# Last FFN of a decoder trunk: gate and value tile as seven products of quarters, and one projection moved

## The chip, the cores and the metric

The kernel runs on one NeuronCore of a Trainium2 chip. The metric is the device time of one launch in microseconds. Engines: PE (TensorE), DVE (VectorE), ACT (ScalarE), POOL (GpSimd), SP (SyncE, which issues the DMAs).

## The reference

One inference step of a two-layer recurrent decoder trunk in float32: model width 1024, 1024 prompt tokens and 8 sample tokens, all with the same weights.

```
for layer in (0, 1):
    x += mixer(rmsnorm(x, norm_mix[layer]))      # layer 0: gated linear attention + retention
                                                 # layer 1: mLSTM + RG-LRU; each ends in ... @ w_out
    g, u = split(rmsnorm(x, norm_ffn[layer]) @ w_up)   # 1024 -> 2 x 2816
    x += (silu(g) * u) @ w_down                        # 2816 -> 1024
y = rmsnorm(x, norm_final)
```

The mixer states of the prompt and of the samples are outputs too.

## The kernel before, in words

Everything is transposed: features on partitions, tokens on the free axis. The tokens are two sets, A (512 prompt tokens) and B (512 prompt tokens and the 8 samples, 520, worked as two pieces of 260 columns, each in a PSUM bank of its own). A tensor of width 1024 is eight tiles of 128 rows.

Every product is split: a float32 operand is a high part (an fp32r copy, by ACT) and a low part (the operand less its high part, by POOL for weights and by DVE for activations), and a product is high x high + high x low + low x high, three matmuls. Weights come in blocks of 128 x 1024 (512 KB) through a ring of four slots: SP fills `wr` (line 594) once the block four before is used, ACT makes `wh` (L1114), POOL `wl` (L1380).

An FFN has 22 hidden tiles, worked as 11 groups of two. A group has four `up` units (gate, value, gate, value; `dense`, L761), each eight k-steps x 3 matmuls, for B x 2 pieces, and then eight `down` units of the group before it (L816), each two k-steps x 3, for B x 2 pieces. A `down` unit is added to `x` by DVE (`accumulate`, L1774). The gate's way: DVE multiplies the PSUM result by the norm's factor `rs` into `sq` (L1550), ACT applies Silu (L1239), POOL multiplies by `rs` once more (L1486), DVE multiplies with the value's PSUM result into `hf` (L1787), ACT makes `hidh` (L1244), DVE `hidl` (L1793). So the normalisation by `rs` comes behind the product: the FFN's input is only x times the gain (`x_split`, L1124 and L1563).

`order()` writes one list of steps by hand; every engine walks this list in order and does what the step means for it. `Plan` gives each PE unit one bank of four (B: an aligned pair of banks) in turn, and PE waits, before it writes, until the bank's last user has been read. A step placed between two others on DVE thus also delays what stands behind it.

Layer 1 before: mixer of A, FFN of layer 0 for B, output projection of A, input projections of B, FFN of A (with the mixer's scans of B between its units), output projection `out` of B (8 units of 48 matmuls, with A's final norm and output beside it), FFN of B. The last group of downs of B goes in two halves of the columns, with the final norm between.

## Time and profile before

| | us |
|---|---|
| median of 3 runs | 2498.04 (2495.83 to 2499.22) |
| the profiled execution | 2493.78 |
| its span, first to last instruction | 2492.0 |
| PE busy | 2432.9 (98%) |
| POOL busy | 1252.7 (50%) |
| DVE busy | 1007.6 (40%) |
| ACT busy | 934.2 (37%) |

Busy time of PE is modelled from pipelined matmuls; its weight loads (PEld) lie beside them. A row of a timeline gives start, duration and instruction, and in brackets how long the engine had been idle and who released it; "x2" is two instructions merged. `xB<-ps,xB` means that xB is written from ps and xB. L1774 is a line of the kernel.

### The profile page before, as it was taken

What the parts mean: (1) busy time and instruction counts of PE and PEld (TensorE: products, weight loads), DVE (VectorE), ACT (ScalarE), POOL (GpSimd) and SP (SyncE); (2) the same over time, 40 slices, a digit from 0 to 9 for tenths busy, and PEclk for the clock granted to TensorE, in tenths of its full rate; (3) what the DMA queues carried; (4) which work ended last, traced back from release to release, by engine and by line L of the source; (5) the groups of instructions that cost most, each with busy time, mean ns of one, the idle gap of its engine ahead of it and who ended that gap; (6) DMA issues with size and microseconds to landing.
All of it is one profiled execution on the core that took longest, in us unless ns stands there. A gap on an engine that the chain in (4) does not pass through costs nothing.

```text
span 2492.0 us, 36702 instructions
## 1 busy us (share of the span) xinstructions
PE 2432.9 (98%) x15510; PEld 2193.5 (88%) x15510; DVE 1007.6 (40%) x1712; ACT 934.2 (37%) x1219; POOL 1252.7 (50%) x669
## 2 busy tenths in 40 slices
PE   8999999899999999999999999999999999999998
PEld 6889987688887877999999889988887889999998
DVE  4513245334445434543333443454434454222224
ACT  5342345233223455443333254544432335222223
POOL 3745455555455644544354473344445556544453
PEclk9999999999999999999999999999999999999999
DMA  5322233321323222222222222222233323222222
GB/s 184 102 82 69 71 130 97 115 77 60 123 85 119 92 90 92 88 74 94 85 77 94 77 88 87 85 95 75 86 101 107 126 86 127 92 88 93 94 85 86
DMA packets 74594, 235.18 MB, mean 94 GB/s; under 512 B 9216, under 2 KB 13120, under 8 KB 74432
## 3 DMA queue, kind: packets, MB, share of 16 engines
q1 hardware_dynamic: 74432, 232.84, 27.9%
q8 instruction: 123, 2.02, 0.3%
q14 instruction: 39, 0.32, 0.0%
HBM read 221.64 MB, written 9.05 MB: 93 GB/s over the span
## 4 chain that ended last, share of the span: by engine, by line
PE 86%; DVE 5%; POOL 2%; issue 2%; ACT 2%; POOLq 1%; DVEq 1%; DMA 1%; SPq 0%; ACTq 0%
PE ps L761 62%; PE ps L816 17%; POOL wl L1380 1%; DMA wr<-in_wblk 1%; PE ps L912 1%; PE ps L910 1%; PE ps L856 1%; ACT wh L1114 1%; PE ps L785 0%; DVE sq L1550 0%; DVE mixl L1764 0%; POOL sq L1486 0%; PE ps L973 0%; POOLq L1397 0%; PE ps L970 0%
## 5 line engine op out<-in xcount | busy, mean ns | idle before, releaser
L1380 POOL TENSOR_TENSOR wl<-wr,wh 128x1024 fp32r<-128x1024 f32 x392 | 943.3, 2420 | 592.2 <-ACT wh L1114 591.7
L761 PE MATMUL ps<-xh,wh 128*128 128x260 f32 (+2 forms) x3296 | 882.5, 322 | 8.1 <-DVE qk L1552 4.2
L761 PE MATMUL ps<-xl,wh 128*128 128x260 f32 (+2 forms) x3296 | 869.0, 318 | 0.0
L761 PE MATMUL ps<-xh,wl 128*128 128x260 f32 (+1 forms) x3280 | 867.1, 319 | 0.0
L761 PEld LDWEIGHTS ps<-xh,wh 128*128 128x128 f32 (+1 forms) x3296 | 544.4, 188 | 61.6 <-issue 18.8
L761 PEld LDWEIGHTS ps<-xl,wh 128*128 128x128 f32 (+1 forms) x3296 | 543.7, 188 | 44.9 <-issue 2.4
L761 PEld LDWEIGHTS ps<-xh,wl 128*128 128x128 f32 x3280 | 541.9, 188 | 44.6
L1114 ACT ACTIVATE wh<-wr 128x1024 fp32r<-128x1024 f32 (+2 forms) x396 | 410.0, 1045 | 393.8 <-DMA wr<-in_wblk 389.2
L816 PE MATMUL ps<-hidh,wh 128*128 128x260 f32 (+1 forms) x1024 | 279.9, 327 | 21.8 <-POOL wl L1380 9.5
L1239 ACT ACTIVATE sq<-sq 128x512 f32<-128x512 f32 (+1 forms) x88 | 55.9, 636 | 609.0 <-DVE sq L1550 609.0
L816 PE MATMUL ps<-hidl,wh 128*128 128x260 f32 (+1 forms) x1024 | 276.3, 323 | 0.0
L816 PE MATMUL ps<-hidh,wl 128*128 128x260 f32 (+1 forms) x1024 | 276.0, 323 | 0.0
L816 PEld LDWEIGHTS ps<-hidh,wh 128*128 128x128 f32 x1024 | 171.9, 190 | 44.3 <-issue 13.7
L1486 POOL TENSOR_TENSOR sq<-sq,rsB 128x520 f32<-128x520 f32 x44 | 60.0, 1364 | 296.7 <-ACT sq L1239 296.7
L1486 POOL TENSOR_TENSOR sq<-sq,rsA 128x512 f32<-128x512 f32 x44 | 57.7, 1312 | 273.6 <-ACT sq L1239 273.5
L1774 DVE TENSOR_TENSOR xB<-ps,xB 128x520 f32<-128x520 f32 x184 | 128.5, 699 | 163.3 <-PE ps L816 107.6
L816 PEld LDWEIGHTS ps<-hidh,wl 128*128 128x128 f32 x1024 | 171.4, 190 | 15.6
L816 PEld LDWEIGHTS ps<-hidl,wh 128*128 128x128 f32 x1024 | 171.7, 190 | 14.1
L1774 DVE TENSOR_TENSOR xA<-ps,xA 128x512 f32<-128x512 f32 x192 | 129.1, 687 | 125.2 <-PE ps L816 75.9
L1787 DVE TENSOR_TENSOR hf<-ps,sq 128x512 f32<-128x512 f32 (+1 forms) x88 | 61.0, 693 | 292.3 <-PE ps L761 278.5
L1244 ACT ACTIVATE hidh<-hf 128x512 fp32r<-128x512 f32 (+1 forms) x88 | 55.8, 634 | 214.7 <-DVE hf L1787 214.7
L1550 DVE TENSOR_TENSOR sq<-ps,rsB 128x520 f32<-128x520 f32 x44 | 30.8, 699 | 186.5 <-PE ps L761 180.4
(373 smaller groups left out, 2316.9 us busy)
## 6 DMA issues: line engine op xcount, KB each, us to landing
wr<-in_wblk SPq DMA_DIRECT2D x392, 512.0 KB, 3.4
xr<-in_xT SPq DMA_DIRECT2D x8, 260.0 KB, 5.8
xB<-in_xT SPq DMA_DIRECT2D x8, 260.0 KB, 5.8
out_yT<-xB SPq DMA_DIRECT2D x8, 260.0 KB, 2.2
xr<-in_xT SPq DMA_DIRECT2D x8, 256.0 KB, 6.0
xA<-in_xT SPq DMA_DIRECT2D x8, 256.0 KB, 4.4
Ss<-in_s_even SPq DMA_DIRECT2D x1, 2048.0 KB, 10.1
out_ss_even<-Ss SPq DMA_DIRECT2D x1, 2048.0 KB, 9.2
```

Source lines behind the costliest of these rows:

```text
L761: mm = pe.matmul(ps[0:cols, b + c, 0:n], wt[:, w], xt[:, e:e + n], start=first, stop=end)
L816: mm = pe.matmul(ps[:, b + c, 0:n], wt[:, w], xt[:, t + lo:t + lo + n], start=first, stop=end)
L856: mm = pe.matmul(ps[:, b + c, 0:n], lhsT, src[0:p, lo:lo + n], start=True, stop=True)
L910: pe.matmul(ob, QZ[X][:, h * C:(h + 1) * C], S[:, (h // 2) * P:(h // 2 + 1) * P], start=True, stop=False)
L1114: act.activation(hi, raw, ACT.Copy).then_inc(s_hi, 1)
L1239: act.activation(t, t, ACT.Silu).then_inc(s_si, 1)
L1244: act.activation(hidh[:, t], hf[:, t], ACT.Copy).then_inc(s_hh, 1)
L1380: pool.tensor_tensor(lo, raw, hi.bitcast(F32), ALU.subtract).then_inc(s_lo, 1)
L1486: pool.tensor_tensor(t, t, rs[X][:], ALU.mult).then_inc(s_sr, 1)
L1550: mm = v.tensor_tensor(cut(dst, X), src, cut(rs[X][:], X), ALU.mult)
L1774: v.tensor_tensor(t, bank(pl.bank[u], X), t, ALU.add).then_inc(s_evd, 1)
L1787: v.tensor_tensor(cut(hf[:, t:t + W[X]], X), bank(pl.bank[u], X), cut(sq[q // 2][:, 0:W[X]], X), ALU.mult).then_inc(s_evd, 1)
```

## The change

Only the last FFN of B and its surroundings change.

- A pair (gate tile and value tile of one hidden tile) is a product of 2 x 2 blocks (gate or value; first or second half of the 1024 inputs) with 2 x 2 blocks (halves of the inputs; halves of the columns). It is worked as seven products of quarters (`sp`), each 4 k-steps x 3 matmuls of 260 columns into one bank, in place of eight. The weights of a pair are a set of eight quarters of 512 columns: two blocks by DMA (`wq`, `weight_set`), four quarters from DVE (`wS`, `set_sums`); seven of the eight are split (`wH`: ACT in four steps `set_hi`, POOL in seven instructions `set_lo`). There are two sets, used in turn. The down blocks have their own slots (`wd` the DMA, `wD` the split).
- The activations are normalised first (`xn`, `scaled`), three more quarters and one changed one come from `xt`, and all seven are split (`xh` by ACT, `xl` by DVE), once for all 22 pairs, during A's last groups.
- Product 0 is copied out by ACT, the others are added by DVE (`products_sum`); the gate's Silu runs on the sum (`gate_sum`), and POOL has no multiplication there.
- B's output projection stands after the ups of group 9 of A's FFN. The mixer tiles are split in another order and earlier. A's final norm, scaling and output go between the pairs of the last FFN.
- The half downs at the end are the same but for the slots of their weights.

```
+LAST = 7
...
+PIECE = (0, 1, 4, 5, 6, 7, 3)
+PSTEP = (0, 0, 1, 1, 2, 2, 3)
+PAIRS = ((0, 2), (4, 6), (6, 8), (3, 4))
 def order():
...
+    def last_ffn(at):
+        for f in range(NF):
+            g, kk = f // 2, f % 2
+            for i in range(7):
+                add(("sp", f, i))
+                if i == 1 and f and (kk or f == 2):
+                    add(("hl", 1, B, (f - 1) // 2, (f - 1) % 2))
+                for s in at.get((f, i), ()):
+                    add(s)
+            add(("hh", 1, B, g, kk))
+            if f + 2 < NF:
+                add(("wq", f + 2))
+            elif f + 2 == NF:
+                add(("wd", NG - 1))
+            if kk and g:
+                for m in range(KT):
+                    add(("down", 1, B, g - 1, m))
+                    if m == 1:
+                        add(("hl", 1, B, g, 1))
+                    for s in at.get((f, "down", m), ()):
+                        add(s)
+                if g + 1 < NG:
+                    add(("wd", g))
...
+    outs = []
+    for m in range(KT):
+        outs.append(("out", 1, B, m))
+        if m:
+            outs.append(("xs", LAST, m - 1))
+    outs += [("xs", LAST, KT - 1), ("wd", 0), ("lnw",)]
+    ffn(1, A, None, merge(rows(B), scan("s1", B, ((0, 2), (0, 4), (1, 0), (1, 2, 3, 4, 5))),
+                          {(6, 1): [("dma", "smp1")], (6, 2): [("u0",)], (7, 0): [("u1",)]},
+                          {p: [("us", 2 * i), ("us", 2 * i + 1)] for i, p in enumerate(((7, 2), (7, 4), (8, 1), (8, 3)))},
+                          {(8, 2): mix(1, B)[4:6], (8, 4): [("ue", 0), ("dma", "smp1out")], (9, 0): [("ue", 1)] + mix(1, B)[6:8],
+                           (9, 1): mix(1, B)[0:2], (9, 2): mix(1, B)[2:4], (9, "end"): outs,
+                           (9, "down", 2): [("nrm", LAST)], (9, "down", 3): [("nrv", LAST)],
+                           (9, "down", 6): [("xn", 0)], (9, "down", 7): [("xn", 1)],
+                           (10, 0): [("xn", 2), ("xn", 3), ("xh", 0)], (10, 1): [("xn", 4), ("xn", 5)],
+                           (10, 2): [("xn", 6), ("xn", 7), ("xh", 1)], (10, 3): [("xt", 0), ("xt", 1)], (10, "end"): [("wq", 0)],
+                           (10, "down", 1): [("xh", 3), ("xh", 2)], (10, "down", 3): [("xt", 2), ("xl", 0)],
+                           (10, "down", 4): [("xh", 4), ("xl", 1)], (10, "down", 5): [("xh", 5), ("wS", 0)],
+                           (10, "down", 6): [("wH", 0, 0), ("xl", 2), ("xh", 6)],
+                           (10, "down", 7): [("wq", 1), ("wH", 0, 1), ("xl", 3)], (NG, "down", 0): [("wH", 0, 2), ("xl", 4)],
+                           (NG, "down", 1): [("wH", 0, 3), ("xl", 5)], (NG, "down", 2): [("xl", 6)],
+                           (NG, "down", 5): [("wS", 1)]}))
+    at = {(0, i): [("wH", 1, i - 1)] for i in (1, 2, 3, 4)}
+    for f in range(2, NF):
+        if f == 2 or f % 2 == 0:
+            at.setdefault((f - 1, 3), []).append(("wS", f))
+            for j, i in enumerate((4, 5, 6)):
+                at.setdefault((f - 1, i), []).append(("wH", f, j))
+            at.setdefault((f, 0) if f == 2 else (f - 1, "down", 0), []).append(("wH", f, 3))
+        elif f == 3:
+            at.setdefault((2, 3), []).append(("wS", f))
+            for j, i in enumerate((4, 5, 6)):
+                at.setdefault((2, i), []).append(("wH", f, j))
+            at.setdefault((3, 0), []).append(("wH", f, 3))
+        else:
+            at.setdefault((f - 2, "down", 3), []).append(("wS", f))
+            for j, m in enumerate((4, 5, 6, 7)):
+                at.setdefault((f - 2, "down", m), []).append(("wH", f, j))
+    at.setdefault((0, 5), []).append(("wD", 0, 0))
+    at.setdefault((0, 6), []).append(("wD", 0, 1))
+    for g in range(1, NG):
+        f = 2 * g + 2 if g + 1 < NG else 2 * g + 1
+        at.setdefault((f, 3), []).append(("wD", g, 0))
+        at.setdefault((f, 5), []).append(("wD", g, 1))
+    for m in range(KT):
+        at.setdefault((4 + m, 2), []).append(("xs", 8, m))
+    at.setdefault((12, 4), []).extend([("nrm", 8), ("nrv", 8)])
+    for m in range(0, KT, 2):
+        at.setdefault((14 + m // 2, 1), []).append(("fin", m))
+        at.setdefault((14 + m // 2, 4), []).append(("fin", m + 1))
+        at.setdefault((14 + m // 2, 6), []).append(("fo", m))
+    last_ffn(at)
...
+            def product(u, f, i):
+                pe.wait_ge(s_qhi, 4 * f + PSTEP[i] + 1)
+                pe.wait_ge(s_qlo, 4 * f + PSTEP[i] + 1)
+                if f == 0:
+                    pe.wait_ge(s_xqh, XQ[i] + 1)
+                    pe.wait_ge(s_xql, i + 1)
+                banks_free(u)
+                b = pl.bank[u]
+                for k in range(KT // 2):
+                    w, e = slice(PIECE[i] * 512 + k * P, PIECE[i] * 512 + (k + 1) * P), slice(k * Q, (k + 1) * Q)
+                    for wt, xt, first, end in ((wqh[f % 2], xqh[i], k == 0, False), (wqh[f % 2], xql[i], False, False),
+                                               (wql[f % 2], xqh[i], False, k == KT // 2 - 1)):
+                        mm = pe.matmul(ps[:, b, 0:Q], wt[:, w], xt[:, e], start=first, stop=end)
+                mm.then_inc(s_unit, 1)
...
+            def quarter_hi(i):
+                act.wait_ge(s_xn, (1, 2, 4, 3, 2, 3, 5)[i])
+                act.activation(xqh[i][:], xqr[i], ACT.Copy).then_inc(s_xqh, 1)
+            def set_hi(f, j):
+                if j in (0, 3):
+                    act.wait_ge(s_wq[f % 2], 32 * (f // 2 + 1))
+                else:
+                    act.wait_ge(s_wsum, f + 1)
+                if (f, j) == (1, 0):
+                    act.wait_ge(s_unit, pl.done(("down", 1, A, NG - 1, KT - 1)))
+                e = slice(512 * PAIRS[j][0], 512 * PAIRS[j][1])
+                act.activation(wqh[f % 2][:, e], wqr[f % 2][:, e], ACT.Copy).then_inc(s_qhi, 1)
+            def down_hi(g, k):
+                act.wait_ge(dslot(g, k, s_wd), 16 * (g + 1) if g < NG - 1 else 16)
+                act.activation(dslot(g, k, dwh)[:], dslot(g, k, dwr)[:], ACT.Copy).then_inc(s_dhi, 1)
+            def first_product(it, f, i):
+                act.wait_ge(s_unit, pl.u[it] + 1)
+                if f:
+                    act.wait_ge(s_evd, pl.evac["sp", f - 1, 4])
+                act.activation(p1[:], ps[:, pl.bank[pl.u[it]], 0:Q], ACT.Copy).then_inc(s_eva, 1)
...
+            def set_lo(f, j):
+                pool.wait_ge(s_qhi, 4 * f + j + 1)
+                pool.wait_ge(s_wsum, f + 1)
+                for n in range(*PAIRS[j]):
+                    e = slice(512 * n, 512 * n + 512)
+                    last = pool.tensor_tensor(wql[f % 2][:, e], wqr[f % 2][:, e], wqh[f % 2][:, e].bitcast(F32), ALU.subtract)
+                last.then_inc(s_qlo, 1)
+            def down_lo(g, k):
+                pool.wait_ge(s_dhi, 2 * g + k + 1)
+                hi, lo, raw = (dslot(g, k, t) for t in (dwh, dwl, dwr))
+                for e in (slice(0, 512), slice(512, 1024)):
+                    last = pool.tensor_tensor(lo[:, e], raw[:, e], hi[:, e].bitcast(F32), ALU.subtract)
+                last.then_inc(s_dlo, 1)
...
+            def scaled(m):
+                kh, k = m // 4, m % 4
+                half = KT // 2 * Q
+                dst = xq[:, 2 * half * kh:2 * half * (kh + 1)].rearrange("p (t c) -> p t c", t=2)[:, :, k * Q:(k + 1) * Q]
+                mm = v.scalar_tensor_tensor(dst, cut(tile(x[B], m, B), B), pcol("gffn1", m), cut(rs[B][:], B), ALU.mult, ALU.mult)
+                if k == 3:
+                    mm.then_inc(s_xn, 1)
+            def quarter_sum(i):
+                v.drain()
+                b11, b12, b21, b22 = xqr[0], xqr[3], xqr[1], xqr[4]
+                if i == 0:
+                    v.tensor_tensor(xqr[5], b22, b12, ALU.subtract)
+                    v.drain()
+                    v.tensor_tensor(b12, b12, b11, ALU.subtract).then_inc(s_xn, 1)
+                elif i == 1:
+                    v.tensor_tensor(xqr[2], b22, xqr[3], ALU.subtract).then_inc(s_xn, 1)
+                else:
+                    v.tensor_tensor(xqr[6], xqr[2], b21, ALU.subtract).then_inc(s_xn, 1)
+            def quarter_lo(i):
+                v.drain()
+                v.wait_ge(s_xqh, XQ[i] + 1)
+                v.tensor_tensor(xql[i][:], xqr[i], xqh[i][:].bitcast(F32), ALU.subtract).then_inc(s_xql, 1)
+            def set_sums(f):
+                a11, a12, a21, a22, s2, s1, s4, s3 = (wqr[f % 2][:, 512 * n:512 * n + 512] for n in range(8))
+                v.drain()
+                v.wait_ge(s_wq[f % 2], 32 * (f // 2 + 1))
+                v.tensor_tensor(s1, a21, a22, ALU.add)
+                v.tensor_tensor(s3, a11, a21, ALU.subtract)
+                v.drain()
+                v.tensor_tensor(s2, s1, a11, ALU.subtract)
+                v.drain()
+                v.tensor_tensor(s4, a12, s2, ALU.subtract).then_inc(s_wsum, 1)
+            def products_sum(it, f, i):
+                if i == 0:
+                    return
+                u = pl.u[it]
+                src = ps[:, pl.bank[u], 0:Q]
+                t = (2 * (f // 2 % 2) + f % 2) * W[B]
+                v.drain()
+                if i == 1:
+                    v.wait_ge(s_eva, pl.evac["sp", f, 0])
+                v.wait_ge(s_unit, u + 1)
+                if i == 1:
+                    v.tensor_tensor(gsum[:, 0:Q], src, p1[:], ALU.add).then_inc(s_evd, 1)
+                elif i == 2:
+                    v.tensor_tensor(usum[:], src, p1[:], ALU.add).then_inc(s_evd, 1)
+                elif i == 3:
+                    v.tensor_tensor(p1[:], src, usum[:], ALU.add)
+                elif i == 4:
+                    v.tensor_tensor(gsum[:, Q:2 * Q], src, p1[:], ALU.add).then_inc(s_evd, 1)
+                elif i == 5:
+                    v.tensor_tensor(usum[:], src, usum[:], ALU.add).then_inc(s_evd, 1)
+                    v.drain()
+                    v.tensor_tensor(hf[:, t + Q:t + 2 * Q], ps[:, pl.bank[pl.u["sp", f, 3]], 0:Q], usum[:], ALU.add).then_inc(s_evd, 1)
+                else:
+                    v.tensor_tensor(hf[:, t:t + Q], usum[:], src, ALU.subtract).then_inc(s_evd, 1)
+                    v.drain()
+                    v.wait_ge(s_gsi, f + 1)
+                    v.tensor_tensor(hf[:, t:t + 2 * Q], hf[:, t:t + 2 * Q], gsum[:], ALU.mult).then_inc(s_hm, 1)
...
+            def weight_set(f):
+                if f == 0:
+                    sp.wait_ge(s_unit, pl.done(("up", 1, A, NG - 1, 3)))
+                elif f == 1:
+                    sp.wait_ge(s_unit, pl.done(("down", 1, A, NG - 2, KT - 1)))
+                else:
+                    sp.wait_ge(s_unit, pl.done(("sp", f - 2, 6)))
+                b = NB + B_FFN + (2 * f if f < 2 else 4 + (f // 2 - 1) * 6 + 2 * (f % 2))
+                for i in range(2):
+                    sp.dma_start(wqr[f % 2][:, i * D:(i + 1) * D], a["wblk"][b + i]).then_inc(s_wq[f % 2], 16)
+            def down_blocks(g):
+                if g == 0:
+                    sp.wait_ge(s_unit, pl.done(("out", 1, B, KT - 1)))
+                elif g < NG - 1:
+                    sp.wait_ge(s_unit, pl.done(("down", 1, B, g - 1, KT - 1)))
+                else:
+                    sp.wait_ge(s_unit, pl.done(("sp", NF - 2, 6)))
+                b = NB + B_FFN + (8 + g * 6 if g < NG - 1 else 4 + (NG - 1) * 6)
+                for i in range(2):
+                    sp.dma_start(dslot(g, i, dwr)[:], a["wblk"][b + i]).then_inc(dslot(g, i, s_wd), 16)
```

## Rows read from the trace of the kernel before

**Rows 1.** The page: busy time by engine, then the chain by engine.
```profile
PE 2432.9 (98%) x15510; PEld 2193.5 (88%) x15510; DVE 1007.6 (40%) x1712; ACT 934.2 (37%) x1219; POOL 1252.7 (50%) x669
...
PE 86%; DVE 5%; POOL 2%; issue 2%; ACT 2%; POOLq 1%; DVEq 1%; DMA 1%; SPq 0%; ACTq 0%
```

**Rows 2.** Windows: length; busy us of PE, PEld, DVE, ACT, POOL; clock; DMA.
```profile
2104.00:2300.00 196.00, 196.00 (x1633) 196.00 (x1632) 53.47 (x77) 51.66 (x60) 93.80 (x45) 1.00 0.27 91
```

**Rows 3.** Waits of PE, 1700 to 2492: total us, times, longest us.
```profile
PE ps L816 <- POOL wl L1380: 1.3, 2, 0.8
PE ps L816 <- DVE xA L1774: 1.3, 1, 1.3
```

**Rows 4.** Timeline of DVE in B's last downs of layer 0: start, duration, instruction.
```profile
1418.42 0.70 DVE L1774 TENSOR_TENSOR xB<-ps,xB 128x520 f32<-128x520 f32 x1 [0.76 <-PE ps L816]
...
1424.22 0.70 DVE L1774 TENSOR_TENSOR xB<-ps,xB 128x520 f32<-128x520 f32 x1 [0.73 <-PE ps L816]
...
1429.21 1.03 DVE L1563 SCALAR_TENSOR_TENSOR xl<-xB,par,xh 128x520 fp32r<-128x520 f32 x1 [2.85 <-ACT xh L1124]
...
1430.78 2.26 DVE L1563 SCALAR_TENSOR_TENSOR xl<-xB,par,xh 128x520 fp32r<-128x520 f32 x1
```

**Rows 5.** Timeline of PE in the same place, idle time in brackets.
```profile
1430.91 0.51 PE L816 MATMUL ps<-hidh,wh 128*128 128x260 f32 x2 [2.39 <-DVE xB L1774]
...
1433.70 0.50 PE L816 MATMUL ps<-hidh,wh 128*128 128x260 f32 x2 [1.10 <-DVE xB L1774]
```

**Rows 6.** DVE groups: L2053 from 2104 on; all `hidl`, minimum/median/maximum ns.
```profile
L2053 DVE TENSOR_TENSOR xB<-ps,xB 128x260 f32<-128x260 f32 x14 | 6.0, 428 | 4.9 <-PE ps L832 4.8
...
L1793 DVE TENSOR_TENSOR hidl<-hf,hidh x88: 678/689/2890, 400.5 to 2458.7; 128x512 fp32r<-128x512 f32 x44, 128x520 fp32r<-128x520 f32 x44
```

**Rows 7.** Groups of ACT, 2104 on: busy us, mean ns, idle before.
```profile
L1114 ACT ACTIVATE wh<-wr 128x1024 fp32r<-128x1024 f32 x63 | 65.3, 1052 | 37.4 <-DMA wr<-in_wblk 37.2
...
L1239 ACT ACTIVATE sq<-sq 128x520 f32<-128x520 f32 x22 | 14.1, 640 | 181.6 <-DVE sq L1550 181.6
...
L1165 ACT ACT_TABLE_LOAD x1 | 1.3, 1283 | 0.1
```

**Rows 8.** Timeline of POOL: one of 512 and three of 1024 behind it.
```profile
1935.47 1.30 POOL L1486 TENSOR_TENSOR sq<-sq,rsA 128x512 f32<-128x512 f32 x1 [11.90 <-ACT sq L1239]
1936.71 7.06 POOL L1380 TENSOR_TENSOR wl<-wr,wh 128x1024 fp32r<-128x1024 f32 x3
```

**Rows 9.** Timelines of DVE and of POOL at one time, 1989.
```profile
1989.15 5.50 DVE L1764 SCALAR_TENSOR_TENSOR mixl<-vm,par,mixh 128x520 fp32r<-128x520 f32 x2 [2.21 <-ACT mixh L1232]
...
1988.88 5.21 POOL L1380 TENSOR_TENSOR wl<-wr,wh 128x1024 fp32r<-128x1024 f32 x2
```

**Rows 10.** Timelines: SP issues two blocks; ACT starts on the second.
```profile
2038.09 0.80 SPq L594 DMA_DIRECT2D wr<-in_wblk  x2
...
2042.76 1.06 ACT L1114 ACTIVATE wh<-wr 128x1024 fp32r<-128x1024 f32 x1 [0.20 <-DMA wr<-in_wblk]
```

**Rows 11.** Timeline of DVE in group 9 of A's last FFN.
```profile
1974.49 0.69 DVE L1550 TENSOR_TENSOR sq<-ps,rsA 128x512 f32<-128x512 f32 x1 [4.77 <-PE ps L761]
...
1982.07 2.27 DVE L2042 TENSOR_TENSOR vm<-oc,gt 128x32 f32<-128x32 f32 x1
...
1985.65 0.69 DVE L1550 TENSOR_TENSOR sq<-ps,rsA 128x512 f32<-128x512 f32 x1 [0.71 <-PE ps L761]
```

**Rows 12.** Timeline of DVE in A's last downs, nine units apart.
```profile
2036.70 0.69 DVE L1774 TENSOR_TENSOR xA<-ps,xA 128x512 f32<-128x512 f32 x1 [0.71 <-PE ps L816]
...
2049.30 0.69 DVE L1774 TENSOR_TENSOR xA<-ps,xA 128x512 f32<-128x512 f32 x1 [0.71 <-PE ps L816]
```

**Rows 13.** Windows around idle stretches of PE; columns as in rows 2.
```profile
405.00:415.00 10.00, 5.29 (x15) 3.37 (x14) 7.90 (x8) 3.06 (x4) 5.24 (x4) 0.69 0.34 97
...
1426.00:1436.00 10.00, 6.52 (x52) 6.09 (x52) 7.15 (x9) 6.88 (x10) 8.16 (x5) 1.00 0.08 33
1543.00:1553.00 10.00, 5.76 (x33) 5.32 (x32) 5.54 (x7) 3.33 (x4) 4.02 (x2) 0.83 0.18 52
```

More of the change, by code:

```diff
@@ L84, in ffn @@
                     add(("nrm", N_FFN[L, X]))
+            for s in at.get((g, "end"), ()):
+                add(s)
             if g:
@@ L87, in ffn @@
                     add(("down", L, X, g - 1, m))
+                    for s in at.get((g, "down", m), ()):
+                        add(s)
                     if m == 1:
@@ L279, in __init__ @@
                 self.rs_end[x[1]] = rs_cur[NORMS[x[1]][0]]
-            if k not in ("sm", "in", "z", "out", "up", "down", "dh", "rg", "s1"):
+            if k not in ("sm", "in", "z", "out", "up", "down", "dh", "rg", "s1", "sp"):
                 continue
@@ L317, in __init__ @@
                 new = [NB * x[1] + B_FFN + (0 if g == 0 else 4 + (g - 1) * 6) + q]
[L318 to L326 removed]
+            elif k == "dh" or k == "down" and x[1:3] == (1, B):
+                continue
             elif k == "down":
```

221 lines of the change are left out of this document (148 added, 73 removed).

## The prediction

> **What bounds the kernel now.** The page's busy line and chain come first: TensorE (PE) is busy 98% of the span and PE is 86% of the chain [rows 1]. The windows by stage show where it is full: in the last FFN of B (2104 to 2460) PE is busy all the time, DVE 27% and POOL 48 to 51% [rows 2]. Over the last 792 us PE waits for POOL and for DVE 1.3 us each, ahead of the tail [rows 3]. So matmuls taken out of that FFN come off the end, but any DVE, ACT or POOL result that arrives late adds to it in full. The question is whether the side engines keep up with seven products.
>
> **What goes.** A pair's gate and value tile are now 2 x 8 k-steps x 3 x 2 pieces = 96 matmuls of 260 columns; seven products of 4 x 3 are 84. Over 22 pairs 264 go. Accumulations of B's downs, 12 such matmuls each, come every 1.45 us (four in 5.80) [rows 4]: 0.121 each, **-31.9 us**. A product takes 1.45 us, a pair 10.16, eight downs 11.6, so a group (even pair, odd pair, downs) 31.9 where it was 34.8. The form (128x260, own weights) is the old one, so I give the rate no doubt.
>
> **Prices of the new side work.** DVE: an add of 260 from PSUM 0.43 [rows 6], one of 520 from PSUM 0.70 [rows 4], one of 512 or 520 from SBUF 0.69 in the median (largest 2.89) [rows 6]. The four sums of 512 in `set_sums` are such SBUF ones; drains between them cost about 0.07, so one call is 0.69 + 0.61 + 0.75 + 0.75 = 2.8 us. A 1040-wide one: 0.70 + 520 x (0.70 - 0.43)/260 = 1.24. ACT: 1024 wide 1.05, 520 wide 0.64, table load 1.28 [rows 7]. POOL: 512 wide 1.30, or 1.24 in a row; 1024 wide 2.35 in a row; a set is 7 of 512, 8.7 us [rows 8].
>
> DVE and POOL also stop each other. Two `mixl` of 520, 1.4 us by themselves, took 5.50 beside two POOL instructions, ending 0.56 us after the second; the POOL pair took 5.21 [rows 9] where 2 x 2.35 and 0.05 are its time. I read: a DVE operation with two SBUF inputs that comes while POOL runs waits for the end of POOL's instruction, then runs, and POOL's next is 0.45 later. Operations that read PSUM keep their 0.69 or 0.70 [rows 4, 12]. By the Trainium skill, "SBUF — State Buffer", section "SBUF: two separate sides", the pair of ports is an exclusive lock held for the whole instruction. The trace agrees on DVE's waiting; by the page POOL would lose the whole 0.69 instead of my 0.45, some 4 us more over the change.
>
> **The steady group, step by step** (zero: product 0 of the even pair starts; a result reaches DVE 0.19 after the last issue).
> Even pair: the fourth sum at 7.5 to 7.9, fifth and its second add end 9.8, before 10.16, when product 0 of the odd pair wants that bank. No stall. Its set's successor is requested by SP at 10.35; two blocks land 4.7 us after the first issue [rows 10]: 15.1.
> Odd pair: product 3 is evacuated 16.2 to 16.6; `set_sums` for the next even set stands right behind it, 16.65 to 19.45, POOL idle. Product 5's second add, which frees the bank of product 3, ends 20.9. Down 0 wants that bank at 20.32: **0.65**. ACT meanwhile is held by the gate's Silu (needs sum 4, 19.95): Silu to 20.65, first high part to 21.7. So POOL starts its 8.7 us of low parts only at 21.7.
> Downs (start D = 21.0): accumulation 3 ends D+6.7. `set_sums` for the odd set stands between accumulations 3 and 4. A down of B uses two of four banks, so down 6 needs accumulation 4. It wants it at D+8.7; behind 2.8 us of sums it gets it at D+10.2: **1.5**, if POOL is silent. It is not: started at D+0.7 and delayed once by `hl` behind down 1, it has two to three instructions left. Sum 1 waits 0.65 for a boundary, sum 2 and the third wait one instruction each (about 1.1 beyond their own time): sums end D+12.1, accumulation 4 at D+12.8, **2.65** more. That such an order stalls PE the trace shows: in B's downs at 1429, an `xl` that came 2.85 us late ahead of an accumulation left PE idle 2.39, the next, stretched to 2.26, left it idle 1.10 [rows 4, 5].
> Together 4.8 per group against 2.9 gained. Odd sets 5, 7, ... 21 stand so: nine groups, **+43.2**. POOL's busy total (11.2 + lock 2.7 per pair of 16) stays below the bound, and the odd set's low parts, 33.2 to 41.9, are in time for 46.9. Bounds: 0 (PE never short) to 9 x 7.2 = 65 (all four sums behind a POOL instruction).
>
> **Entry into the last FFN.** Four terms:
> - B's output projection after group 9's ups. The mixer tiles 0 to 3 wait for the sample chain, whose last write ends 1984.3 [rows 11]. Then `mixl` 6, 7, `hf`, `mixl` 0, 1, `sq`, `hl` put `mixl` 2 and 3 behind POOL's two `wl` of that place [rows 9]: they end at 1994.7 and 1997.5. The ups come every 5.58 us (1974.49, 1985.65), so PE starts the projection at 1991.1 and wants them at 1992.5 and, after the first wait, 1995.4: **+4.3**. The two waits of 1.3 us of the downs there [rows 3] go, their weights being long ready: **-2.6**. Bounds -2.6 to +8. The 8 projections are the same 384 matmuls; their `xh` and `xl` (ACT, DVE) go, their squares stay; nothing waits on the longer A phase. The norm comes during downs 2 to 4 and is in time.
> - The hand-over A to B. From the end of A's last up (T), downs are 16 x 1.40 = 22.4 us [rows 12]. DVE has there: 3 + 1 quarter operations and seven `xl` of 1.24, `set_sums` 2.8 twice, `hl`, 16 accumulations. A's four banks let PE run 4 ahead. In order, accumulations 4, 5, 6, 7 end T+13.1, 15.0, 18.5, 20.9; 8 to 11, each behind an `xl` that waits for one POOL low part, 23.3, 25.7, 28.1, 30.5. PE ends at T+32.0: 9.6 late, 0.4 more at product 2: **+10**. (7 without the lock; 14 if the first sums wait for full `wl` too.)
> - Sets 2 and 3 have no downs before them. From product 3's result of the pair before: evacuation 0.43, sums 2.8, sum 4 0.5, Silu 0.64, high part 1.05, two low parts 2.5 = 7.95 us, where three products less the latency give 4.2. **+3.75 and +3.85**.
> - A's final norm at pair 12: DVE waits behind sum 4 for Silu, two table loads of 1.28 and two passes of 0.64 [rows 7]: to 12.5, the second add to 13.45 where 10.16 is wanted: **+3.3**. Two of A's eight final scalings stand behind `set_sums` of odd pairs (15, 17): 2 x 0.7 = **+1.4**. In bounds 0 to 6 together. Their output DMAs have SP idle around them.
>
> Edits at nothing: A's squares (ACT 0.63, POOL 1.3 a pair, pairs 4 to 11) lie where both idle; the tail (half downs) has the same instructions, its down blocks are two pairs ahead.
>
> **Sum.** 43.2 + 4.3 - 2.6 + 10 + 7.6 + 3.3 + 1.4 = 67.2 lost, 31.9 gained: **+35.3**. The profiled execution took 2493.8 (span 2492.0): 2529.1, span 2527.3. The median of the runs, 2498.0, lies 4.3 above it, so 2533.
>
> **Rivals.**
> 1. Order alone (no lock on the sums, as if POOL were through): nine groups at 2.15 = 19.4, hand-over 7; the rest as above. 40.4 lost: +8.5, 2507 (2498 to 2515). For it: `hidl` is 0.69 in the median beside a POOL that is half idle [rows 2, 6]; against it: POOL here starts just before. It decides where POOL's low parts end before D+6.7.
> 2. Faster: the seven products win. The side work is hidden in the groups, PE loses only at entry and at the norm, some 17 us: -15, 2483. For it: DVE has 73% idle now. It decides where `set_sums` delays accumulation 4 by less than 1.4 us. Against it: four sums can't be shorter than 2.4, and two banks give 1.4.
> 3. The clock: stalls of 2 us or more bring PE to half rate. Of six windows of 10 us around idle stretches of 2 to 4.7 us, five have a mean granted clock of 0.69 to 0.83, so 3.4 to 6.2 us at the lower of the two levels, 1.2 GHz; one, with 2.4 and 1.1 idle, has 1.00 [rows 13]. At half rate 3.4 us do the work of 1.7; at some 8 of the long stalls +13: 2546. By the Trainium skill, "TensorE: Matmul & The Clock Gate", section "Part 1: The HAM clock gate", the low clock is the default and activity lifts it; this trace's falls behind idle stretches agree.
>
> **Chances.** Forecast 0.50 (own range 2515 to 2545), order alone 0.20, faster 0.20, clock 0.10. What a measurement of this kernel can tell from no change is about 0.2%, 5 us. Order alone reaches down into that band, 0.08 of it. So faster 0.20, same 0.08, slower 0.72. The range goes from 2485, inside the faster case, to 2558, the clock case with its upper bounds.
>
> **What the profile after would show.** PE matmuls 15246; PE idle up by some 60 us. Right if PE's waits show nine of about 4 us on `xB`'s accumulation at down 6 of B and nine below 1 us at down 0; the four sums of a call in the downs stretched to over 5 us, those in products 2.8; PE waiting on `xA`'s accumulation near the end of A's FFN, 9 us; two waits near 3.8 on the low parts of sets 2 and 3. Wrong if accumulation 4 follows 3 by under 3 us, if the groups are 32 us apart, or if POOL is the releaser of most waits: then it is a set that is late, not the bank.

## The result and the profile after

The changed kernel takes 2565.24 us (median of 4 runs, 2564.09 to 2566.78), the kernel before 2496.93 beside it (4 runs, 2494.30 to 2499.22): ratio 1.0282, interval 1.0270 to 1.0295. It is 2.8% slower. The forecast was 2533 with a range to 2558: the direction is right, the size is not, and the time lies 7 us outside the range. The profiled execution took 2566.8 us (span 2565.0, mean granted clock 0.979, where it was 0.992).

The page of the kernel after, busy line and chain by engine:

```profile
PE 2437.8 (95%) x15246; PEld 2190.3 (85%) x15246; DVE 1161.9 (45%) x1943; ACT 975.2 (38%) x1286; POOL 1340.9 (52%) x779
...
PE 78%; DVE 9%; issue 3%; POOL 3%; DVEq 2%; ACT 2%; POOLq 2%; DMA 1%; ACTq 0%; SPq 0%
```

The 264 matmuls are gone (15246 for 15510), yet PE is busy 4.9 us longer than in [rows 1]. At 0.121 us each, its busy time should have fallen by 32. So 37 us have come in on other accounts. Most of it is the clock (sized below), since the form of the matmuls is unchanged. A smaller part comes from the way in which busy time is modelled: a matmul stands 0.28 us in the timeline and the next starts after 0.12, so each new idle stretch adds some 0.16, and there are about 40 more of them. In the chain PE has gone from 86% to 78%, and DVE from 5% to 9%.

The waits of PE from 1900 us to the end (total us, times, longest us), kernel after:

```profile
PE ps L999 <- DVE xB L2087: 34.6, 10, 3.9
PE ps L968 <- POOL wql L1625: 9.0, 2, 4.6
PE ps L999 <- DVE hf L1873: 8.4, 9, 1.4
PE ps L999 <- DVE xA L2087: 7.1, 9, 1.9
PE ps L913 <- DVE mixl L2077: 3.7, 2, 2.3
PE ps L968 <- DVE hf L1873: 2.6, 1, 2.6
PE ps L1028 <- POOL rsB L1645: 1.2, 1, 1.2
```

L999 is a down, L968 a product of quarters, L913 a projection. Each line but the last, the tail's, is a step of the prediction: down 6 of B nine times (the tenth wait is a short one), the sets 2 and 3, down 0 nine times, the hand-over from A to B, B's output projection, pair 13. The whole view adds to 68.3 us, against 3.0 in the same view of the kernel before (1.3 for `xA`, 0.5 for `wl` and the tail's 1.2; [rows 3] begin at 1700 us and hold one more wait for `wl`, of 0.8, which the kernel after has too).

A down block in close view. DVE, from accumulation 3 to accumulations 4 and 5, and POOL at the same time (start, duration):

```profile
2176.31 0.70 DVE L2087 TENSOR_TENSOR xB<-ps,xB 128x520 f32<-128x520 f32 x1 [0.47 <-PE ps L999]
2177.10 1.09 DVE L1844 TENSOR_TENSOR wqr<-wqr 128x512 f32<-128x512 f32 x1
2178.11 1.77 DVE L1845 TENSOR_TENSOR wqr<-wqr 128x512 f32<-128x512 f32 x1
2179.95 1.59 DVE L1847 TENSOR_TENSOR wqr<-wqr 128x512 f32<-128x512 f32 x1
2181.62 0.69 DVE L1849 TENSOR_TENSOR wqr<-wqr 128x512 f32<-128x512 f32 x1
2182.23 1.30 DVE L2087 TENSOR_TENSOR xB<-ps,xB 128x520 f32<-128x520 f32 x2
```
```profile
2174.63 6.37 POOL L1625 TENSOR_TENSOR wql<-wqr,wqh 128x512 fp32r<-128x512 f32 x4
2182.46 2.52 POOL L1625 TENSOR_TENSOR wql<-wqr,wqh 128x512 fp32r<-128x512 f32 x2 [1.46 <-DVE wqr L1849]
```

Three sums meet a POOL instruction and are stretched to 1.09, 1.77 and 1.59 us; the fourth comes when POOL has run out of work (2181.0) and takes its own 0.69. The call lasts 5.2 us (4.9 to 5.6 over the nine groups; the calls for the even sets 4 to 20, among the products, take the forecast 2.8), accumulation 4 ends at 2182.9, and PE starts down 6 at 2182.98 after 3.82 us of idle time. POOL's four splits took 6.37 where 5.0 is their time, so it lost about 0.45 to each of three sums.

What the prediction's sum did not hold is seen in windows around two such waits (length; busy us of PE, PEld, DVE, ACT, POOL; granted clock):

```profile
2176.00:2183.00 7.00, 3.18 (x28) 2.98 (x26) 6.45 (x7) 0.70 (x2) 5.54 (x5) 0.94 0.00 0
2182.00:2182.50 0.50, 0.00 (x0) 0.00 (x0) 0.50 (x2) 0.15 (x1) 0.04 (x1) 0.72 0.00 0
2182.50:2183.00 0.50, 0.02 (x1) 0.02 (x1) 0.50 (x2) 0.50 (x1) 0.50 (x1) 0.50 0.00 0
2183.00:2190.00 7.00, 7.00 (x36) 7.00 (x37) 1.93 (x3) 1.87 (x3) 7.00 (x7) 0.57 0.09 13
2190.00:2210.00 20.00, 19.25 (x161) 19.07 (x160) 10.94 (x20) 6.38 (x10) 8.47 (x7) 1.00 0.28 102
2216.00:2223.00 7.00, 3.07 (x25) 2.87 (x25) 6.76 (x7) 0.75 (x1) 5.54 (x5) 1.00 0.01 2
2223.00:2230.00 7.00, 7.00 (x46) 7.00 (x47) 1.83 (x3) 2.68 (x5) 7.00 (x7) 0.76 0.22 61
...
2117.00:2565.00 448.00, 383.06 (x2898) 375.81 (x2898) 265.63 (x401) 149.09 (x207) 275.91 (x209) 0.92 0.23 81
```

Behind the wait that ends at 2183, PE gets 36 matmuls done in 7 us, where 58 would fit at 0.121; behind the next, 46. The granted clock falls to the lower level (1.2 GHz) near the end of a wait: here at 2182.2, 0.8 us before PE starts again at 2182.98, behind the next wait 0.3 us after it has started. Over the thirteen waits of 2 us or more it began 0.1 to 1.7 us before the start eight times and 0.1 to 0.3 after it five times. The stretch there lasts 6.8 us (eight times) or 3.4 (five times), in turn over the ten waits from 2183 on. In it a matmul starts every 0.217 us in place of 0.121. A mean of 0.92 over the last 448 us makes some 70 us at the lower level. [Rows 2] had 1.00 for this FFN. The rule cited in the prediction ("TensorE: Matmul & The Clock Gate" in the Trainium skill, section "Part 1: The HAM clock gate", activity lifts the clock and its absence loses it) is what these rows show. There are fifteen such stretches after 1900 us. Thirteen stand at the thirteen waits of 2 us or more, and none at the 21 shorter ones of 0.3 us and more. One is in the tail, where the kernel before has one too. One, of 3.4 us at 1943, stands behind no wait: PE was busy 18.00 of the 18 us before it. Every kernel with the projection moved has one or two such in that place, the kernel before has none; why is open.

### The profile page after: what moved, and what is told of

It reads as the page before. It is cut to its first block, busy times and chain, and to the rows that moved or that the text cites. A ratio compares the mean times of both kernels' runs of the same rounds, so it can differ in the third digit from the quotient of the medians.

```text
span 2565.0 us, 37014 instructions
## 1 busy us (share of the span) xinstructions
PE 2437.8 (95%) x15246; PEld 2190.3 (85%) x15246; DVE 1161.9 (45%) x1943; ACT 975.2 (38%) x1286; POOL 1340.9 (52%) x779
## 4 chain that ended last, share of the span: by engine, by line
PE 78%; DVE 9%; issue 3%; POOL 3%; DVEq 2%; ACT 2%; POOLq 2%; DMA 1%; ACTq 0%; SPq 0%
PE ps L913 49%; PE ps L999 16%; PE ps L968 6%; POOL wl L1606 1%; DVE wqr L1847 1%; DVEq L1846 1%; DVE wqr L1844 1%; POOLq L1611 1%; DMA wr<-in_wblk 1%; DVE wqr L1849 1%; PE ps L1094 1%; PE ps L1092 1%; ACT wh L1298 1%; DVE xB L2087 1%; PE ps L1038 1%
## 5 line engine op out<-in xcount | busy, mean ns | idle before, releaser
L1606 POOL TENSOR_TENSOR wl<-wr,wh 128x1024 fp32r<-128x1024 f32 x326 | 785.9, 2421 | 569.4 <-ACT wh L1298 568.8
L913 PE MATMUL ps<-xh,wh 128*128 128x260 f32 (+3 forms) x2592 | 740.8, 333 | 8.4 <-DVE qk L1798 4.2
L913 PE MATMUL ps<-xl,wh 128*128 128x260 f32 (+3 forms) x2592 | 727.6, 328 | 0.0
L913 PE MATMUL ps<-xh,wl 128*128 128x260 f32 (+1 forms) x2576 | 725.8, 329 | 0.0
L913 PEld LDWEIGHTS ps<-xh,wh 128*128 128x128 f32 (+1 forms) x2592 | 436.0, 188 | 62.3 <-issue 18.6
L913 PEld LDWEIGHTS ps<-xl,wh 128*128 128x128 f32 (+1 forms) x2592 | 435.4, 187 | 45.0 <-issue 2.4
L913 PEld LDWEIGHTS ps<-xh,wl 128*128 128x128 f32 x2576 | 433.6, 188 | 44.7
L1625 POOL TENSOR_TENSOR wql<-wqr,wqh 128x512 fp32r<-128x512 f32 x154 | 215.1, 1432 | 106.8 <-ACT wqh L1344 85.7
L999 PE MATMUL ps<-hidh,wh 128*128 128x512 f32 (+1 forms) x704 | 215.4, 346 | 29.1 <-DVE xA L2087 10.6
L999 PE MATMUL ps<-hidl,wh 128*128 128x512 f32 (+1 forms) x704 | 211.2, 340 | 0.0
L999 PE MATMUL ps<-hidh,wl 128*128 128x512 f32 (+1 forms) x704 | 210.7, 340 | 0.0
L968 PE MATMUL ps<-xqh,wqh 128*128 128x260 f32 x616 | 178.5, 290 | 12.2 <-POOL wql L1625 9.0
L968 PE MATMUL ps<-xql,wqh 128*128 128x260 f32 x616 | 177.3, 288 | 0.0
L968 PE MATMUL ps<-xqh,wql 128*128 128x260 f32 x616 | 177.1, 287 | 0.0
L999 PEld LDWEIGHTS ps<-hidh,wh 128*128 128x128 f32 x704 | 121.5, 189 | 53.5 <-issue 14.9
L999 PEld LDWEIGHTS ps<-hidh,wl 128*128 128x128 f32 x704 | 121.3, 189 | 15.5
L999 PEld LDWEIGHTS ps<-hidl,wh 128*128 128x128 f32 x704 | 121.6, 190 | 14.0
```

Source lines behind the costliest of these rows:

```text
L913: mm = pe.matmul(ps[0:cols, b + c, 0:n], wt[:, w], xt[:, e:e + n], start=first, stop=end)
L968: mm = pe.matmul(ps[:, b, 0:Q], wt[:, w], xt[:, e], start=first, stop=end)
L999: mm = pe.matmul(ps[:, b + c, 0:n], wt[:, w], xt[:, t + lo:t + lo + n], start=first, stop=end)
L1606: pool.tensor_tensor(lo, raw, hi.bitcast(F32), ALU.subtract).then_inc(s_lo, 1)
L1625: last = pool.tensor_tensor(wql[f % 2][:, e], wqr[f % 2][:, e], wqh[f % 2][:, e].bitcast(F32), ALU.subtract)
```

## The experiments

Times are medians, each beside runs of the kernel before on the same chip: 2496.27 us for experiments 1 to 4, 2494.20 for 5 to 7, 2495.06 for 8 and 9, 2495.32 for 10 and 11. PE's waits are those from 1900 us on.

**1. The waits kept, the clock held up.** PE runs matmuls that nothing reads, into a bank that is free there, in the time in which it waits anyway:

```diff
+            def filler(n):
+                for _ in range(n):
+                    pe.matmul(ps[:, 4, 0:Q], xqh[0][:, 0:P], xqh[0][:, 0:Q], start=True, stop=True)
 def product(u, f, i):
+                if i == 0 and f in (2, 3, 13):
+                    filler(18 if f == 13 else 36)
 def down(u, L, X, g, m):
+                if (L, X) == (1, B) and g < 9 and m in (0, 6):
+                    filler(30 if m else 5)
```

> Changed kernel with extra matmuls whose results nobody reads, put where TensorE otherwise waits in the last FFN: 30 before down 6 and 5 before down 0 of nine groups, 36 before product 0 of pairs 2 and 3, 18 before that of pair 13. At 0.12 us each they fit into the waits of 4.1, 0.9, 4.7 and 2.7 us. Theory (the unexplained 40 us are mostly the granted clock falling after each wait): the clock stays at 1.00 over the last FFN, the waits stay where they are, and the time falls from 2565 by 25 to 30 us, to about 2538. Rival (the 40 us are work that got slower for another reason): no change, 2565, or somewhat more where a filler doesn't fit.

2540.93 us, ratio 1.0179 (1.0162 to 1.0196). 24.3 us came back. Windows over B's FFN (first row this kernel, second row the kernel after):

```profile
2104.00:2500.00 396.00, 386.31 (x3125) 377.90 (x3124) 254.10 (x369) 136.52 (x182) 278.75 (x202) 1.00 0.24 86
```
```profile
2104.00:2525.00 421.00, 363.31 (x2721) 354.88 (x2720) 253.60 (x368) 136.57 (x182) 276.57 (x202) 0.92 0.23 81
```

The side engines did the same work (DVE 254.1 and 253.6 us, POOL 278.8 and 276.6), the clock stood at 1.00, and the FFN ended 25 us sooner with some 400 matmuls more (the edit adds 405). So about 24 us of the loss is the clock, lost at the waits. The waits at the entry were not filled, and two of them still have their stretch at the lower clock.

**2. The sums of the odd set after the last down.** In `order`:

```diff
-            at.setdefault((f - 2, "down", 3), []).append(("wS", f))
-            for j, m in enumerate((4, 5, 6, 7)):
-                at.setdefault((f - 2, "down", m), []).append(("wH", f, j))
+            at.setdefault((f - 2, "down", 7), []).append(("wS", f))
+            for j in range(4):
+                at.setdefault((f - 1, j), []).append(("wH", f, j))
```

> Changed kernel with the sums of the odd sets 5, 7, ... 21 after down 7 instead of down 3, and the split of that set in steps at products 0 to 3 of the next pair. Theory (DVE's order holds the bank of down 6): the nine waits of 4.1 us go, 37 us, and with them some 10 to 15 us of half clock; down 0 still waits 0.9. About 2517. Rival (POOL is short of time, so the set is late whatever the order): the wait moves to product 0 of the odd pair, with POOL's low part as releaser; gain under 10 us, 2555 or more.

2543.64 us, ratio 1.0192 (1.0177 to 1.0207), between the two. The wait at down 6 is gone, so the sums between two accumulations were its cause. But the wait has moved to down 0. The first line of PE's waits, then DVE and POOL during the sums of the even set, which this edit left where they were:

```profile
PE ps L999 <- DVE hf L1873: 30.7, 9, 4.6
```
```profile
2200.54 0.75 DVE L1844 TENSOR_TENSOR wqr<-wqr 128x512 f32<-128x512 f32 x1
2201.21 1.78 DVE L1845 TENSOR_TENSOR wqr<-wqr 128x512 f32<-128x512 f32 x1
2203.07 1.62 DVE L1847 TENSOR_TENSOR wqr<-wqr 128x512 f32<-128x512 f32 x1
2204.76 1.60 DVE L1849 TENSOR_TENSOR wqr<-wqr 128x512 f32<-128x512 f32 x1
```
```profile
2197.74 6.40 POOL L1632 TENSOR_TENSOR dwl<-dwr,dwh 128x512 fp32r<-128x512 f32 x4
2204.30 1.51 POOL L1617 TENSOR_TENSOR rsA<-rsA,sq 128x512 f32<-128x512 f32 x1 [0.16 <-issue]
```

POOL's splits slid later with the odd set and now run beside the even sums, which stretch from 2.8 to 5.8 us (4.7 to 6.5 in seven of nine). The odd sums, now beside an idle POOL, take 0.69 each. The stretch thus goes with POOL's work, not with the place of the sums: that is the lock, shown from both sides.

**3. The even sums one product earlier, the odd sums untouched.**

```diff
         if f == 2 or f % 2 == 0:
+            if f > 2:
+                at.setdefault((f - 1, 2), []).append(("wS", f))
+                for j, i in enumerate((3, 3, 4, 5)):
+                    at.setdefault((f - 1, i), []).append(("wH", f, j))
+                continue
             at.setdefault((f - 1, 3), []).append(("wS", f))
...
```

> Changed kernel with the sums of the even sets 4 to 20 behind product 2 instead of 3 of the odd pair, and the split one step earlier. The odd sets' sums stay after down 3. Theory (order plus the lock between DVE and POOL): down 0 no longer waits (8 us), and since POOL ends its low parts 3 us earlier the four sums at down 3 take about 3 us in place of 4.7: down 6 waits 1.5 to 2.3 in place of 4.1, 16 to 23 us, with some 10 us of half clock besides; about 2530. Rival (order alone, the lock costs nothing): down 6 waits as before, only the 8 us go, 2557.

2531.40 us, ratio 1.0142 (1.0127 to 1.0157): the theory of order and lock together gave 2530, order alone 2557. POOL starts earlier here and is through sooner, and the sums in the downs, though in the same place as before, meet it once instead of three times (start, duration on DVE):

```profile
2210.51 1.29 DVE L1849 TENSOR_TENSOR wqr<-wqr 128x512 f32<-128x512 f32 x1
2211.72 0.68 DVE L1850 TENSOR_TENSOR wqr<-wqr 128x512 f32<-128x512 f32 x1
2212.48 0.69 DVE L1852 TENSOR_TENSOR wqr<-wqr 128x512 f32<-128x512 f32 x1
2213.24 0.69 DVE L1854 TENSOR_TENSOR wqr<-wqr 128x512 f32<-128x512 f32 x1
```
```profile
PE ps L1004 <- DVE xB L2092: 16.7, 10, 1.9
```

34.6 us of waits at down 6 became 16.7 in ten, 1.7 in the mean and 1.9 at most. The prediction had split 4.15 into 1.5 for the order and 2.65 for the lock; with one sum of four still held up 0.6 us, the order's own share comes out between 1.1 and 1.7.

**4. No sums at all.** The four sums are left out and the quarters filled by a second pair of transfers, so the output is not the reference's:

```diff
-                for i in range(2):
-                    sp.dma_start(wqr[f % 2][:, i * D:(i + 1) * D], a["wblk"][b + i])...
+                for i in range(4):
+                    sp.dma_start(wqr[f % 2][:, i * D:(i + 1) * D], a["wblk"][b + i % 2])...
-                v.tensor_tensor(s1, a21, a22, ALU.add)
...
+                v.sem_inc(s_wsum, 1)
```

> Changed kernel with the four sums of every set left out: the quarters are filled by a second pair of DMAs instead, so the products use other weights and the output is not the reference's. Theory (what is lost in the last FFN is what waits behind the sums): no waits at down 0 and down 6, pairs 2 and 3 wait about 1.8 in place of 4.6, half clock mostly gone; 37 + 8 + 6 + 20 to 25 less, about 2492. Rival (POOL or ACT bounds the groups): waits for low parts appear instead, 2520 or more.

2499.75 us, ratio 1.0016 (1.0006 to 1.0025). The waits at down 6 and down 0 are all but gone (2.5 us on `xB`, 0.7 on `hf`), so the sums carry 65 of the 68 us between the two kernels' times, with what the clock made of them. What is left waits at the entry, at the sets 2 and 3 and at pair 13. The expectation was 8 us too low, and the result says something that the prediction did not: even without the sums the change as a whole, the move of the projection with it, does not win. The next runs look for the rest.

**5. The projection moved, nothing else.** The kernel before with B's output projection between groups 9 and 10 of A's FFN:

```diff
-         (A, None), (B, "gffn1"), (B, None))
+         (B, "gffn1"), (A, None), (B, None))
...
+                        (9, 1): mix(1, B)[0:2], (9, 2): mix(1, B)[2:4], (9, "end"): outs}))
```

> Kernel before with the second part of the change alone: B's output projection after the ups of group 9 of A's last FFN, the mixer tiles split in the new order and earlier, A's final norm and output among B's first groups. All products as before. Theory: it costs the wait for mixer tiles 2 and 3 (4 us) less the 2.6 us of the downs there, so 2496 to 2502, no change that can be told. Rival (the move itself brings a good part of the loss, by POOL and DVE work pushed onto A's groups): 2510 or more.

2510.02 us, ratio 1.0064 (1.0047 to 1.0080), 16 us slower where 2496 to 2502 was expected. PE's waits of this kernel:

```profile
PE ps L773 <- POOL wl L1392: 4.6, 1, 4.6
PE ps L773 <- DVE mixl L1775: 3.9, 2, 2.3
PE ps L828 <- DVE xB L1785: 1.8, 2, 1.1
```

The two waits for `mixl` are the term that the prediction priced at 4.3. The 4.6 at 2119 stands in this kernel alone: the high parts of B's first weights (ACT) are behind A's squares and three table loads of the norms. The lower clock costs another 6 us by my count. The wait of 4.6 with the slow stretch at its end (about 7 us) and the 1.8 on `xB` stand in this kernel alone. The waits for `mixl`, with the lower clock at 1943 and 1998, are met in the changed kernel too: some 7 of the 16 us.

**6. The four sums as four steps.** In the odd pair's set one sum each behind downs 3, 4, 5 and 6; in the even pair's set behind products 2, 2, 3 and 4:

```diff
...
-            at.setdefault((f - 2, "down", 3), []).append(("wS", f))
+            for p in range(4):
+                at.setdefault((f - 2, "down", 3 + p), []).append(("wS", f, p))
...
```

> Changed kernel with the four sums of each set from 4 on as four separate steps: odd sets behind downs 3, 4, 5 and 6, even sets behind products 2, 2, 3 and 4 of the odd pair; the splits follow. Same instructions, same lock. Theory (a run of sums ahead of one accumulation is what costs, one sum fits into the 0.75 us that DVE has between two): the waits at down 0 and down 6 (43 us together) go to under 5 in all, the half clock behind them goes too (about 20): 2500 to 2505. Rival (the lock makes even one sum too long, or POOL has no room for 7 + 4 instructions a pair): small waits at most downs or waits for low parts, 2525 or more.

2516.48 us, ratio 1.0087 (1.0072 to 1.0102), 11 to 16 us above the expectation. Two of PE's waits:

```profile
PE ps L1008 <- DVE hf L1885: 13.5, 8, 2.5
PE ps L1008 <- DVE xB L2099: 0.2, 1, 0.2
```

The waits at down 6 fell from 34.6 us to 0.2, with the lock still there: a single sum between two accumulations, even one of 1.2 us, fits into the 1.45 and the spare bank. At down 0, 13.5 us are left where the expectation had under 5 for both downs together; the 9.3 for low parts are as before.

**7. The same, with the other places mended.** Sets 2 and 3 a product earlier, A's final norm in two steps, `xl` spread over the hand-over, and B's projection beginning with the mixer tiles 4 to 7, which are ready first:

```diff
...
-                for k in range(KT):
+                ks = (4, 5, 6, 7, 0, 1, 2, 3) if src[0] is mixh[1, B] else range(KT)
+                for k in ks:
...
-    at.setdefault((12, 4), []).extend([("nrm", 8), ("nrv", 8)])
+    at.setdefault((12, 4), []).append(("nrm", 8))
+    at.setdefault((13, "down", 2), []).append(("nrv", 8))
```

> The same, and: sums of sets 2 and 3 behind product 2 with the high part ahead of the gate's Silu; A's final norm awaited at down 2 behind pair 13; three of the seven low quarters and the sums of set 1 spread over A's last downs and pair 0; B's projection takes the mixer tiles in the order 4 to 7, 0 to 3. Theory: 9 us at pairs 2 and 3 fall to 2, 2.7 at pair 13 to 0, 7 at the hand-over to about 3, 4 at the projection to 1.5, and half clock with them: some 20 us below the spread version, 2482, so faster than the kernel before by 0.6%. Rival (waits move rather than go): level with the spread version or within 8 us of it, no faster than the kernel before.

2502.60 us, ratio 1.0036 (1.0026 to 1.0047). 14 us better than the one before, and 20 short of the expectation. The waits for `mixl` fell to 1.5, those for `xA` to 3.8, those for low parts to 3.9, pair 13's is gone; down 0 has 15.2 in 8, no less than before.

**8 and 9. Two tries at POOL's order.** First A's squares moved from the products into downs 5 and 6 of four pairs:

```diff
-        at.setdefault((4 + m, 2), []).append(("xs", 8, m))
+        at.setdefault((5 + m // 2 * 2, "down", 5 + m % 2), []).append(("xs", 8, m))
```

> The best version so far with A's squares (ACT and one POOL addition of 1.5 us each) moved from product 2 of pairs 4 to 11 to downs 5 and 6 of pairs 5, 7, 9 and 11. Theory (what still waits, 2 us at down 0 of eight groups, are sums of the even set stretched by POOL instructions that run beside them): in the four groups with squares down 0 waits about 1 us less, 4 us in all, 2498 in place of 2502. Rival (the sums' number, not the lock, holds the bank of product 3): no change.

2503.44 us, ratio 1.0036 (1.0022 to 1.0050): no change, as the rival said, but its reason is not shown. The lock was not gone. In one of the four groups the even sums meet POOL no more, and down 0 waits 1.2 us in place of 2.2; in the other three they still meet its splits, and the waits are 1.9 to 2.1 where they were 1.7 to 2.5. Then the second block of down weights split later too:

```diff
-        at.setdefault((f, 5), []).append(("wD", g, 1))
+        at.setdefault((f + 1, 3) if g + 1 < NG else (f, 5), []).append(("wD", g, 1))
```

> In addition the second down block's split moved from product 5 of the even pair to product 3 of the odd pair, so that POOL is silent while three of the four even sums run. Theory: these sums take 0.7 each in place of 1.0 to 1.8, down 0 waits under 0.5 us in place of 2, 12 to 15 us less than e_best, 2488: faster than the kernel before by 0.3%. Rival (POOL then has too little room ahead of down 0): down 0 waits for the low part of the down block, about 2 us each, and the time stays at 2498 to 2502.

2538.96 us, ratio 1.0171 (1.0158 to 1.0185), badly missed, though the even sums from set 6 on do take 0.69 us each as expected. PE's first wait, and POOL at down 0 (here 2271.5):

```profile
PE ps L1011 <- POOL dwl L1644: 40.3, 8, 5.5
```
```profile
2265.98 2.49 POOL L1637 TENSOR_TENSOR wql<-wqr,wqh 128x512 fp32r<-128x512 f32 x2 [5.17 <-DVE wqr L1864]
2268.43 2.94 POOL L1644 TENSOR_TENSOR dwl<-dwr,dwh 128x512 fp32r<-128x512 f32 x2
2271.34 3.76 POOL L1637 TENSOR_TENSOR wql<-wqr,wqh 128x512 fp32r<-128x512 f32 x3
```

The split of the downs' weights ends at 2271.3, and down 0 needs it 5 us earlier. POOL had been idle for 5.17 us before, waiting for the next set's sums: in its queue the splits of that set stand first. A program's order on an engine with 53% load left it idle and late at once.

**10 and 11. The even sums together again, at two places.** From version 7 (which the expectation calls the spread version), all four behind product 2; and two behind product 1, two behind 2. The cut shows the first, without the steps of the split that follow:

```diff
-                for p, i in enumerate((2, 2, 3, 4)):
-                    at.setdefault((f - 1, i), []).append(("wS", f, p))
+                for p in range(4):
+                    at.setdefault((f - 1, 2), []).append(("wS", f, p))
...
```

> The spread version with one edit: the four even sums stand together behind product 2 of the odd pair, in place of one behind products 2, 2, 3 and 4 each. The version with the even sums together had 0.6 to 0.9 us of wait at down 0 per group where the spread version has 2.0 to 2.7, since there the sums stand between the readings of the last products' banks. Theory: the down-0 waits fall by 1.2 us in eight groups, about 10 us, and the time to 2490-2494, just under the kernel before (0.2% faster). Rival: the sums take the same vector-engine time beside GpSimd's splits wherever they stand, the readings of the last products are as late, and the time stays at 2500-2504.

> The same with the four even sums two behind product 1 and two behind product 2 of the odd pair. Theory: another 0.5 us a group off down 0 if the two quarters have landed by then, 2486-2490. Rival: they land 1.2 us later than product 1's reading (the version with the sums behind product 2 already shows 1.18 us of waiting for the DMA), the first sum then holds the vector engine's queue, PE waits for the banks of products 2 to 4, and the time is 2500-2510.

2499.47 us, ratio 1.0015 (1.0006 to 1.0024), and 2502.30, ratio 1.0029 (1.0018 to 1.0041). The first is the best version of the change: 3 us better than version 7 by the medians, 5 by the ratios, where 10 were expected, because down 0 still waits 13.0 us in eight: 1.3 to 1.7 in five groups, 2.7 in two, 0.5 in one. DVE in one of the five, and a row from one of the two:

```profile
2182.94 0.43 DVE L1880 TENSOR_TENSOR usum<-ps,p 128x260 f32<-128x260 f32 x1
2184.65 0.69 DVE L1858 TENSOR_TENSOR wqr<-wqr 128x512 f32<-128x512 f32 x1 [1.28 <-DMA wqr<-in_wblk]
2185.26 0.69 DVE L1860 TENSOR_TENSOR wqr<-wqr 128x512 f32<-128x512 f32 x1
2186.02 0.69 DVE L1862 TENSOR_TENSOR wqr<-wqr 128x512 f32<-128x512 f32 x1
2186.79 0.69 DVE L1864 TENSOR_TENSOR wqr<-wqr 128x512 f32<-128x512 f32 x1
2187.57 0.43 DVE L1882 TENSOR_TENSOR p<-ps,usum 128x260 f32<-128x260 f32 x1
...
2351.98 1.77 DVE L2377 SCALAR_TENSOR_TENSOR xA<-xA,par,rsA 128x512 f32<-128x512 f32 x1
```

In the first, DVE's queue is held 1.28 us for the two transfers, and the readings of the products behind the sums start late. That is one cause of three: of nine calls, DVE waits for the transfers ahead of three (1.3, 0.5 and 0.6 us), other calls are stretched by POOL (to 4.3 us), and the two waits of 2.7 stand where two of A's final scalings share DVE with the sums. The two groups with none of the three (2320 and 2424) wait 0 and 0.5. Putting the sums earlier (the second kernel) makes the wait for the transfers longer, up to 1.9 us.

## Why the prediction was right in direction and wrong in size

**The gain.** 264 matmuls at 0.121, -31.9: the count is right. That the rate of the form stayed was right at the full clock only.

**The steady group.** Down 6: 4.15 predicted; in PE's waits seven of 3.8 to 3.9 and two of 3.5 were measured (3.8 to 4.2 from start to start of matmuls). Down 0: 0.65 predicted, 0.9 in the mean (8.4 in 9), with three of the nine over the 1 us that was named. Two of these are the scalings of A's output behind the pairs 15 and 17, priced at 1.4 together: down 0 waits 1.4 there and 0.75 in most others. The call of sums in the downs: over 5 us predicted, 4.9 to 5.6 measured. The two mechanisms were tested apart: experiment 2 took the sums out from between the accumulations, and experiment 3 took most of the lock away and left the order. The rival "order alone" fell with experiment 3; the rival "faster", which asked for a delay of accumulation 4 under 1.4 us, fell with the waits.

**The entries.** B's projection 4.3, measured 3.7. Of the 2.6 to be saved there only 1.8 went: the 1.3 for `wl` in [rows 3] were two waits, and the one of 0.8 lies ahead of 1900 us and stayed. The hand-over 10, measured 7.1 in nine waits, and 10.6 with the short gaps that the view of waits does not list. Sets 2 and 3 7.6, measured 9.0. The norm at pair 13 3.3, measured 2.6. All of it is within 3 us a term.

**The sum of the waits.** 67.2 net predicted. The view shows 68.3 less 3.0. From starts of matmuls, where short gaps count too, I make 77.3 less 4.6 = 72.7 from 1900 us on, 5.5 more than predicted.

**The step that failed is the clock, priced at nothing in the sum.** It stood in the prediction as rival 3 alone, with a chance of 0.10, though five of the six windows of [rows 13], three of them printed there, had the lower level at such waits: with thirteen places of 2 us or more forecast in the same text (down 6 nine times, B's projection, two sets, pair 13), it was a term and not a rival. It was also sized too low: "some 8 of the long stalls" at 1.7 us, +13, counted only part of them, each with the shorter stretch. The trace shows a stretch at every one of the thirteen, eight of them the longer one, and some 10 of their 72 us lie inside the waits. Of the rest 44% is lost (0.217 us a matmul for 0.121). Matmuls that started at the lower level took 27.5 us more than at the full one (my sum over 281 of them), 2.1 a wait, and experiment 1 gave back 24.3. Net: 35.3 predicted, 5.5 short gaps, 27.5 clock make 68.3; the spans differ by 73.0. The 4.7 us left are not assigned. With 24 to 28 us in the sum, the forecast would have been 2557 to 2561 us.

**What was not predicted at all** is how little is to be had when all is mended. In the best version PE's waits are still 26 us, its gaps are 28 us above those before, and 10 us go to the lower clock, against 31.9 gained. Experiment 4, without sums, ends in the same place. The forecast of "faster, if the side work is hidden" (2483) priced only the entry and the norm. Moving the projection alone costs 16 us, where the sum had 1.7 net; some 7 of them are met in the changed kernel too, and the best version is 4 us behind the kernel before. I tried no version in which the seven products stand without that move, so whether they would win there is open.
